# The tile's h in two PSUM banks, and all products of the up rows on TensorE in two further banks

## The chip, the cores and the metric

The kernel runs on one NeuronCore of a Trainium2 chip. The number is the device time of one execution in microseconds (us), lower is better. Engines are named as in the profile: PE is TensorE (PEld its weight loads), DVE is VectorE, ACT is ScalarE, POOL is GpSimd, SP is SyncE, which here only issues DMAs. All data is float32 unless a line says otherwise.

## The reference

Two blocks of a network run one after the other on 256 tokens of width 1024. The first block has two layers; a layer works on a sequence x and, in the first layer, also on a context of 256 tokens. Each ends in a lookup of experts (`_peer`), and that is the part the change touches. Every token picks 8 x 16 = 128 of 16384 experts, multiplies its vector h with each picked row of `peer_down`, and sums the picked rows of `peer_up`, weighted by gate and gelu:

```python
def one(args):
    hh, ee, gg = args
    a = jnp.einsum("tkd,td->tk", peer_down[ee], hh, preferred_element_type=jnp.float32)
    act = (gg * jax.nn.gelu(a)).astype(hh.dtype)
    return jnp.einsum("tk,tkd->td", act, peer_up[ee])
```

`ee` (token, 128) are the expert numbers from two top-16 searches per head, one over 128 + 128 scores and one over their 256 sums; `gg` is a softmax over the 16 best. The result is multiplied by a modulation vector and added to x. Around it stand an attention with 8 heads, a Fourier and a pooling branch, gates and output products. The second block (feed-forward, convolution, attention, feed-forward) follows the lookup and is not touched.

## The kernel before, in words

**Work and order.** A pass of one sequence through one layer is a run: `x0` and `c0` are sequence and context in layer 0, `x1` and `c1` in layer 1. `ORDER` is a list of stages written by hand; every engine walks the same list and does its share of each stage. There are six gathers, one per run (`x0`, `c0`, `x1`) and tile of 128 tokens (t = 0, 1), numbered G = 0 to 5. Each lasts 16 groups. Between the groups of a gather `ORDER` places stages of something else (beside): ranking, all of `c0` up to its scoring beside `x0`; the modulation of layer 1 (two 1 MB weight loads per group), ranking and the first stages of `x1` beside `c0`; ranking only beside `x1` t = 0, nothing beside `x1` t = 1.

**A group** handles 8 of a token's 128 experts. `rows` has eight slots of 128 x 1024. GpSimd's queue fetches eight rows of `peer_down` (one per token and slot, line 2079, 512 KB each), then eight of `peer_up`, into the same slots: down of group n, up of group n - 1, down of group n + 1 and so on. Before a down row goes into slot j, the up row there must have been used (`upv_done` and `upp_done`); before an up row goes there, the down row must have been used (`down_done`).

- VectorE, per group n: eight reductions of row times h (line 1643, one multiply-and-sum of 1024 elements each, counts `down_done`), three small operations for gelu, the stages beside, then eight accumulations of the left half of the up rows of group n - 1 into `accv` (line 1660, columns 0 to 511, counts `upv_done`), then `act8` of group n, for which it waits for ScalarE's tanh.
- ScalarE: eight diagonal matrices of `act8` of group n - 1 (line 1261, in four buffers `diag`, so each waits for the product four rows earlier), then its beside stages, then tanh of group n (line 1265).
- TensorE: the products of stages beside, then the right half of the up rows of group n - 1: `diag` times row, columns 512 to 1023, summed in PSUM bank 4 over the whole gather (line 847, counts `upp_done`). A float32 product shows as two passes in the trace.

At the end of a gather `fin` multiplies both halves with `mb`, the modulation vector that ScalarE has copied from PSUM, and adds them to x: four operations of 512 elements (lines 1697 to 1701). The next gather begins with a memset of `accv`.

**PSUM** has 8 banks of 512 float32 per partition. Bank 4 (`UPB`) holds the sum; every other product takes the next of the seven banks in `ROT` (`job`) and waits for the engine that empties it (`bank_free`). The attention of `c0` puts the scores of each tile (128 x 256) and each tile's transposed probabilities in a bank of its own.

## Time and profile before

| what | value |
|---|---|
| median of 3 runs | 4579.39 us (4568.43 to 4579.72) |
| profiled execution | 4569.33 us |
| its span on the core | 4567.2 us |
| PE, DVE busy | 3093.4 us, 2899.1 us |
| ACT, POOL busy | 961.5 us, 1820.7 us |
| mean granted TensorE clock | 0.821 of full |
| HBM read | 1153.99 MB, 253 GB/s over the span |

The page gives busy times over the whole span. The gathers run from about 434 us to 2310 us and from 2550 us to 3372 us, with the first stages, a stretch of modulation and layer 1, and the second block around them. Because stages with different limits alternate within a gather, the profile is best read in windows that begin with a group's first reduction on VectorE (line 1643). The granted clock is given as a part of 2.4 GHz; 0.50 is 1.2 GHz. A TensorE busy time is longer at the lower clock for the same work.

### The profile page before, as it was taken

What the parts mean: (1) busy time and instruction counts of PE and PEld (TensorE: products, weight loads), DVE (VectorE), ACT (ScalarE), POOL (GpSimd) and SP (SyncE); (2) the same over time, 40 slices, a digit from 0 to 9 for tenths busy, and PEclk for the clock granted to TensorE, in tenths of its full rate; (3) what the DMA queues carried; (4) which work ended last, traced back from release to release, by engine and by line L of the source; (5) the groups of instructions that cost most, each with busy time, mean ns of one, the idle gap of its engine ahead of it and who ended that gap; (6) DMA issues with size and microseconds to landing.
All of it is one profiled execution on the core that took longest, in us unless ns stands there. A gap on an engine that the chain in (4) does not pass through costs nothing.

```text
span 4567.2 us, 42252 instructions
## 1 busy us (share of the span) xinstructions
PE 3093.4 (68%) x12636; PEld 1964.9 (43%) x12636; DVE 2899.1 (63%) x5798; ACT 961.5 (21%) x1932; POOL 1820.7 (40%) x1732
## 2 busy tenths in 40 slices
PE   5996366688745544566788543344459878898789
PEld 2575022354511111123446311111139768797687
DVE  2215987566788777666642888776666566565365
ACT  1301012111111001111131111111123353333333
POOL 0001566566566555667620477777830000000000
PEclk7998677888867777787899766677679989999799
DMA  5434788899988888899943688899965504454244
GB/s 208 177 135 168 247 295 328 304 365 364 349 288 320 306 338 302 323 359 354 396 166 115 205 306 308 326 346 349 348 260 186 173 32 170 166 184 168 83 166 152
DMA packets 273573, 1157.15 MB, mean 253 GB/s; under 512 B 30848, under 2 KB 31616, under 8 KB 234496
## 3 DMA queue, kind: packets, MB, share of 16 engines
q0 software_dynamic: 221184, 805.40, 48.3%
q1 hardware_dynamic: 52224, 349.75, 21.2%
q8 instruction: 78, 1.28, 0.1%
q14 instruction: 87, 0.71, 0.0%
HBM read 1153.99 MB, written 1.05 MB: 253 GB/s over the span
## 4 chain that ended last, share of the span: by engine, by line
PE 40%; DVE 24%; DMA 20%; issue 9%; POOL 4%; ACT 2%; POOLq 0%; DVEq 0%; SPq 0%; ACTq 0%
DMA rows<-in_peer_up,iup 13%; PE ps L886 7%; PE ps L887 7%; PE ps L888 7%; DVE rows L1643 6%; DVE accv L1660 6%; DMA rows<-in_peer_down,idown 5%; PE ps L847 5%; POOL rows L2079 3%; PE ps L773 3%; PE ps L615 3%; PE ps L818 2%; PE ps L796 1%; PE ps L991 1%; DVE shared L1594 1%
## 5 line engine op out<-in xcount | busy, mean ns | idle before, releaser
L847 PE MATMUL ps<-rows,diag 128*128 128x512 f32 x1536 | 1021.3, 792 | 1182.7 <-DMA rows<-in_peer_up,iup 1139.9
L847 PEld LDWEIGHTS ps<-rows,diag 128*128 128x128 f32 x1536 | 320.2, 239 | 1864.3 <-DMA rows<-in_peer_up,iup 1336.6
L2079 POOL DMA_INDIRECT rows<-in_peer_down,idown x768 | 866.9, 1129 | 532.0 <-DVE accv L1660 269.3
L2079 POOL DMA_INDIRECT rows<-in_peer_up,iup x768 | 883.2, 1150 | 345.9 <-issue 185.1
L1660 DVE SCALAR_TENSOR_TENSOR accv<-rows,act,accv 128x512 f32<-128x512 f32 x768 | 577.4, 752 | 336.1 <-DMA rows<-in_peer_up,iup 295.7
L1261 ACT ACTIVATE diag<-ident,act 128x128 f32<-128x128 f32 x768 | 277.4, 396 | 2104.9 <-PE ps L847 1605.6
L1643 DVE CUSTOM_DVE_ANT_0 rows<-rows,h_in 128x1024 f32<-128x1024 f32 x512 | 612.3, 1225 | 89.2 <-DMA rows<-in_peer_down,idown 76.1
L886 PE MATMUL ps<-hT_hi,w_hi 128*128 128x256 f32 x1600 | 452.9, 283 | 16.5 <-DVE hT_lo L1758 16.5
L887 PE MATMUL ps<-hT_hi,w_lo 128*128 128x256 f32 x1600 | 452.9, 283 | 0.0
L888 PE MATMUL ps<-hT_lo,w_hi 128*128 128x256 f32 x1600 | 450.6, 282 | 0.0
L1643 DVE CUSTOM_DVE_ANT_0 rows<-rows,h_ctx 128x1024 f32<-128x1024 f32 x256 | 310.9, 1225 | 110.9 <-DMA rows<-in_peer_down,idown 106.3
L1745 DVE TENSOR_TENSOR w_lo<-wring,w_hi 128x2048 fp32r<-128x2048 f32 x120 | 275.0, 2292 | 142.9 <-ACT w_hi L1308 141.4
L886 PEld LDWEIGHTS ps<-hT_hi,w_hi 128*128 128x128 f32 x1600 | 306.2, 191 | 18.1 <-issue 18.1
L2084 POOL COPY idown<-idx 128x8 uint32 (+1 forms) x96 | 40.3, 420 | 666.7 <-DVE gates L1629 666.4
L887 PEld LDWEIGHTS ps<-hT_hi,w_lo 128*128 128x128 f32 x1600 | 304.0, 190 | 0.0
L888 PEld LDWEIGHTS ps<-hT_lo,w_hi 128*128 128x128 f32 x1600 | 303.9, 190 | 0.0
L1308 ACT ACTIVATE w_hi<-wring 128x2048 fp32r<-128x2048 f32 x120 | 229.4, 1912 | 130.4 <-DMA wring<-in_wdn 82.6
L773 PE MATMUL ps<-hT,wring 128*128 128x256 f32 x1152 | 253.0, 381 | 0.0
L773 PEld LDWEIGHTS ps<-hT,wring 128*128 128x128 f32 x1152 | 219.9, 191 | 38.2 <-issue 8.1
L818 PE MATMUL ps<-hT,wring 128*128 128x256 f32 x768 | 168.9, 379 | 2.0 <-ACT hT L1089 2.0
L818 PEld LDWEIGHTS ps<-hT,wring 128*128 128x128 f32 x768 | 144.8, 190 | 22.8 <-issue 3.9
L887 PE MATMUL ps<-w_hi,hid_lo 128*128 128x512 f32 x352 | 138.3, 393 | 0.0
(274 smaller groups left out, 3700.4 us busy)
## 6 DMA issues: line engine op xcount, KB each, us to landing
wring<-in_wgu SPq DMA_DIRECT2D x66, 1024.0 KB, 4.8
wring<-in_wmod SPq DMA_DIRECT2D x48, 1024.0 KB, 7.9
wring<-in_wG SPq DMA_DIRECT2D x36, 1024.0 KB, 7.8
wring<-in_wdn SPq DMA_DIRECT2D x33, 1024.0 KB, 4.8
wring<-in_wpq SPq DMA_DIRECT2D x24, 1024.0 KB, 5.7
rows<-in_wgu SPq DMA_DIRECT2D x22, 1024.0 KB, 4.8
wring<-in_wO SPq DMA_DIRECT2D x12, 1024.0 KB, 4.9
wring<-in_wout SPq DMA_DIRECT2D x12, 1024.0 KB, 4.8
```

What stands on the lines that cost most here:

```text
L773: last = pe.matmul(b[:, dt * TOK:(dt + 1) * TOK], w[:, k * 256 + dt * P:k * 256 + (dt + 1) * P], hT[:, k, :], start=(k == 0), stop=(k == K ...
L818: last = pe.matmul(b[:, hp * TOK:(hp + 1) * TOK], w[:, k * 256 + hp * P:k * 256 + (hp + 1) * P], hT[:, k, :], start=(k == 0), stop=(k == K ...
L847: pe.matmul(ps[:, UPB, :], diag[:, j % DIAGS, :], rows[:, j, UPV:D], start=(first and j == 0), stop=(last and j == GROUP - 1), skip_group_ ...
L886: pe.matmul(out_, lh[l_at], rh[r_at], start=start, stop=False)
L887: pe.matmul(out_, ll[l_at], rh[r_at], start=False, stop=False)
L888: return pe.matmul(out_, lh[l_at], rl[r_at], start=False, stop=stop)
L1261: act.activation(diag[:, j % DIAGS, :], ident[:, :], ACT.Copy, scale=act8[:, j:j + 1]).then_inc(diag_ready, 1)
L1308: act.activation(W2_HI[c % SLOTS2], W2[c % SLOTS2], ACT.Copy).then_inc(hi_ready, 1)
L1643: dve.tensor_tensor_reduce(out=rows[:, j, :], in0=rows[:, j, :], in1=h[s][:, t, :], scale=1.0, scalar=0.0, op0=ALU.mult, op1=ALU.add, accu ...
L1660: dve.scalar_tensor_tensor(accv[:, :], rows[:, j, 0:UPV], act8[:, j:j + 1], accv[:, :], ALU.mult, ALU.add).then_inc(upv_done, 1)
L1745: dve.tensor_tensor(W2_LO[c % SLOTS2], w, W2_HI[c % SLOTS2].bitcast(f32), ALU.subtract).then_inc(lo_ready, 1)
L2079: pool.indirect_dma_start(out=rows[:, j, :], out_offset=None, in_=table, in_offset=bass.IndirectOffsetOnAxis(ap=offs[:, j:j + 1], axis=0)) ...
```

## The change

Four things change at once. (1) ScalarE copies h of the tile into PSUM banks 6 and 7 (`h_ps`) at the start of a gather, and VectorE's reduction reads h from there. (2) TensorE multiplies both halves of an up row, into banks 4 and 5 (`up_sum`); VectorE's accumulation, `accv` and `upv_done` are gone, and `upp_done` alone frees a slot. (3) `fin` works on 1024 elements at a time, in two operations instead of four. (4) From the start of the first gather to the end of the fourth, and from the start of the fifth on, four banks are left for the stages beside (`ROT_GATHER`); the attention of `c0` therefore puts both tiles' scores in one bank and both tiles' transposed probabilities in one, with one maximum operation and one copy for both instead of two each.

```diff
         ROT = [0, 1, 2, 3, 5, 6, 7]
+        ROT_GATHER = [0, 1, 2, 3]
         UPB = 4
-        UPV = 512
+        TAKEN = [4, 5, 6, 7]
+        up_sum = ps[:, 4:6, :].rearrange("p b n -> p (b n)")
+        h_ps = ps[:, 6:8, :].rearrange("p b n -> p (b n)")
...
             def job(key):
-                b = ROT[rot[0] % len(ROT)]
+                b = banks[0][rot[0] % len(banks[0])]
...
                         pe.wait_ge(diag_ready, 8 * g + (P * G + j + 1))
-                        pe.matmul(ps[:, UPB, :], diag[:, j % DIAGS, :], rows[:, j, UPV:D], start=(first and j == 0), stop=(last and j == GROUP - 1),
-                                  skip_group_check=True).then_inc(upp_done, 1)
-
+                        for half in range(2):
+                            ins = pe.matmul(ps[:, UPB + half, :], diag[:, j % DIAGS, :], rows[:, j, half * 512:(half + 1) * 512],
+                                            start=(first and j == 0), stop=(last and j == GROUP - 1), skip_group_check=True)
+                        ins.then_inc(upp_done, 1)
+
+                if n0 == 0 and run != "c0" and t == 0:
+                    for b in TAKEN:
+                        taken_at[run, b] = uses[b]
+                        uses[b] += 1
+                    banks[0] = ROT_GATHER
...
+                if n0 == 0:
+                    s = RUNS[run][0]
+                    if G in (0, 4):
+                        taken(act, run, TAKEN[2:4])
+                    else:
+                        act.wait_ge(down_done, P * G)
+                    act.wait_ge(mark["h"], norm_mark(run, 1, 2))
+                    for half in range(2):
+                        at_evac(act, ("bh", run, 1, half))
+                    for half in range(2):
+                        cols = slice(half * 512, (half + 1) * 512)
+                        act.activation(h_ps[:, cols], h[s][:, t, cols], ACT.Copy).then_inc(h_copied, 1)
...
+                if nk == 2:
+                    b = at_mm(dve, ("s", run, i)).rearrange("p (t n) -> p t n", t=TT)
+                    c = 2 * (i % 2)
+                    dve.tensor_reduce(nmax[:, c:c + 2], b, axis=AX.X, op=ALU.max, negate=True).then_inc(mark["nmax"], 2)
...
-                if n0 == 0:
-                    v(dve.memset(accv[:, :], 0.0))
 
                 def down(g, first=False):
 
+                    if first:
+                        dve.wait_ge(h_copied, 2 * G + 2)
                     for j in range(GROUP):
                         dve.wait_ge(row_in[j], (16 * (32 * G + 1)) if first else 32 * g + 16 * (32 * G))
-                        dve.tensor_tensor_reduce(out=rows[:, j, :], in0=rows[:, j, :], in1=h[s][:, t, :], scale=1.0, scalar=0.0,
+                        dve.tensor_tensor_reduce(out=rows[:, j, :], in0=rows[:, j, :], in1=h_ps, scale=1.0, scalar=0.0,
                                                  op0=ALU.mult, op1=ALU.add, accum_out=a8[:, j:j + 1]).then_inc(down_done, 1)
...
-                def up(g, last=False):
-                    for j in range(GROUP):
-                        dve.wait_ge(row_in[j], (16 * (32 * G + 32)) if last else 32 * g + (16 * (32 * G + 3)))
-                        if isinstance(g, int) and g == 0 and j == 0:
-                            dve.wait_ge(act_ready, GROUPS * G + 1)
-                        else:
-                            dve.wait_ge(upv_done, 8 * g + (P * G + j))
-                        dve.scalar_tensor_tensor(accv[:, :], rows[:, j, 0:UPV], act8[:, j:j + 1], accv[:, :], ALU.mult, ALU.add).then_inc(upv_done, 1)
-
...
-                dve.wait_ge(upv_done, P * (G + 1))
-                v(dve.tensor_tensor(accv[:, :], accv[:, :], mb[:, 0:UPV], ALU.mult))
                 dve.wait_ge(upp_done, P * (G + 1))
-                v(dve.tensor_tensor(mb[:, UPV:D], ps[:, UPB, :], mb[:, UPV:D], ALU.mult))
-                v(dve.tensor_tensor(x[s][:, t, 0:UPV], x[s][:, t, 0:UPV], accv[:, :], ALU.add))
-                dve.tensor_tensor(x[s][:, t, UPV:D], x[s][:, t, UPV:D], mb[:, UPV:D], ALU.add).then_inc(mark["fin"], 1)
+                v(dve.tensor_tensor(mb[:, :], up_sum, mb[:, :], ALU.mult))
+                dve.tensor_tensor(x[s][:, t, :], x[s][:, t, :], mb[:, :], ALU.add).then_inc(mark["fin"], 1)
                 at_mark(dve, "fin", run, t + 1)
+                if run != "x0" and t == TT - 1:
+                    for b in TAKEN:
+                        dve.sem_inc(bank_free[b], 1)
```

What stands in a row on the engines, at the places where it changes. On TensorE in the first gather, rows 2 to 6 of the first group's up products before, and rows 2 to 4 now; `diag_ready` and `row_in2` are the semaphores of the diagonal and of the fetched row.

```order
308 L847 MATMUL ps<-rows,diag 128x512 [waits diag_ready,row_in2]
309 L847 MATMUL ps<-rows,diag 128x512 [waits diag_ready,row_in3]
310 L847 MATMUL ps<-rows,diag 128x512 [waits diag_ready,row_in4]
311 L847 MATMUL ps<-rows,diag 128x512 [waits diag_ready,row_in5]
312 L847 MATMUL ps<-rows,diag 128x512 [waits diag_ready,row_in6]
```

```order
310 L872 MATMUL ps<-rows,diag 128x512 [waits diag_ready,row_in2]
311 L872 MATMUL ps<-rows,diag 128x512
312 L872 MATMUL ps<-rows,diag 128x512 [waits diag_ready,row_in3]
313 L872 MATMUL ps<-rows,diag 128x512
314 L872 MATMUL ps<-rows,diag 128x512 [waits diag_ready,row_in4]
315 L872 MATMUL ps<-rows,diag 128x512
```

Every row of `peer_up` now has two products, and only the second tells the others that its slot is free. On VectorE at the end of the last gather, from the last group's gelu to its `act8`, before and now (line 1666 waits for ScalarE's tanh):

```order
3985 L1651 TENSOR_TENSOR g<-g,a 128x8 [waits gelu_step]
3986 L1660 SCALAR_TENSOR_TENSOR accv<-rows,act,accv 128x512 [waits upv_done,row_in0]
3987 L1660 SCALAR_TENSOR_TENSOR accv<-rows,act,accv 128x512 [waits upv_done,row_in1]
3988 L1660 SCALAR_TENSOR_TENSOR accv<-rows,act,accv 128x512 [waits upv_done,row_in2]
3989 L1660 SCALAR_TENSOR_TENSOR accv<-rows,act,accv 128x512 [waits upv_done,row_in3]
3990 L1660 SCALAR_TENSOR_TENSOR accv<-rows,act,accv 128x512 [waits upv_done,row_in4]
3991 L1660 SCALAR_TENSOR_TENSOR accv<-rows,act,accv 128x512 [waits upv_done,row_in5]
3992 L1660 SCALAR_TENSOR_TENSOR accv<-rows,act,accv 128x512 [waits upv_done,row_in6]
3993 L1660 SCALAR_TENSOR_TENSOR accv<-rows,act,accv 128x512 [waits upv_done,row_in7]
3994 L1666 SCALAR_TENSOR_TENSOR g<-th,a 128x8 [waits gelu_th]
3995 L1672 TENSOR_TENSOR act<-g,gates 128x8 [waits upv_done,diag_ready,gelu_step]
```

```order
3297 L1711 TENSOR_TENSOR g<-a 128x8 [waits down_done]
3298 L1713 TENSOR_SCALAR g<-g 128x8 [waits gelu_step]
3299 L1715 TENSOR_TENSOR g<-g,a 128x8 [waits gelu_step]
3300 L1721 SCALAR_TENSOR_TENSOR g<-th,a 128x8 [waits gelu_th]
3301 L1726 TENSOR_TENSOR act<-g,gates 128x8 [waits diag_ready,gelu_step]
3302 L1747 TENSOR_TENSOR mb<-ps,mb 128x1024 [waits bank_free1,upp_done,bank_free0,act_ready]
```

The eight accumulations are gone, and VectorE comes to the wait for tanh right after gelu. On ScalarE between the fifth and the sixth gather, before and now (lines 1261 and 1306 are the diagonals, 1089 and 1124 the copy of `mb`):

```order
551 L1261 ACTIVATE diag<-ident,act 128x128 [waits upp_done,act_ready]
552 L1261 ACTIVATE diag<-ident,act 128x128 [waits upp_done] x7
553 L1089 ACTIVATE mb<-ps 128x512 [waits mm_done] x2
554 L1265 ACTIVATE th<-g 128x8 [waits gelu_in]
555 L1261 ACTIVATE diag<-ident,act 128x128 [waits upp_done,act_ready]
```

```order
561 L1306 ACTIVATE diag<-ident,act 128x128 [waits upp_done,act_ready]
562 L1306 ACTIVATE diag<-ident,act 128x128 [waits upp_done] x7
563 L1124 ACTIVATE mb<-ps 128x512 [waits mm_done] x2
564 L1323 ACTIVATE ps<-h_in 128x512 [waits bank_free2,bank_free3,h,down_done]
565 L1323 ACTIVATE ps<-h_in 128x512
566 L1310 ACTIVATE th<-g 128x8 [waits gelu_in]
```

Two copies of h have come between the copy of `mb` and the first tanh of the next gather.

## Rows read from the trace of the kernel before

**Rows 1.** The page: busy shares, then costly groups (busy us, mean ns | idle before).
```profile
PE 3093.4 (68%) x12636; PEld 1964.9 (43%) x12636; DVE 2899.1 (63%) x5798; ACT 961.5 (21%) x1932; POOL 1820.7 (40%) x1732
...
L2079 POOL DMA_INDIRECT rows<-in_peer_down,idown x768 | 866.9, 1129 | 532.0 <-DVE accv L1660 269.3
...
L1660 DVE SCALAR_TENSOR_TENSOR accv<-rows,act,accv 128x512 f32<-128x512 f32 x768 | 577.4, 752 | 336.1 <-DMA rows<-in_peer_up,iup 295.7
```
**Rows 2.** Windows, groups 1 to 14 of each gather: length, busy us, clock, DMA, GB/s.
```profile
469.00:875.50 406.50, 219.68 (x451) 81.60 (x452) 318.34 (x725) 64.93 (x203) 268.10 (x249) 0.71 0.84 294
944.50:1371.00 426.50, 308.99 (x950) 178.80 (x948) 302.64 (x647) 61.39 (x171) 266.45 (x256) 0.83 0.91 341
1436.20:1868.80 432.60, 229.36 (x440) 72.06 (x440) 308.05 (x652) 47.22 (x140) 260.18 (x249) 0.73 0.85 322
1928.80:2289.00 360.20, 238.01 (x640) 122.24 (x640) 236.44 (x432) 61.64 (x179) 252.62 (x254) 0.81 0.95 368
2579.10:2954.40 375.30, 155.47 (x224) 47.31 (x224) 312.65 (x688) 42.41 (x130) 270.39 (x249) 0.67 0.87 307
3003.20:3339.80 336.60, 155.43 (x224) 46.22 (x224) 230.52 (x407) 41.97 (x127) 271.33 (x253) 0.69 0.95 348
```
**Rows 3.** Windows, single groups: PE, PEld, DVE, ACT, POOL, clock, DMA, GB/s.
```profile
595.50:625.40 29.90, 12.36 (x16) 3.44 (x16) 27.98 (x83) 2.98 (x9) 18.78 (x18) 0.61 0.81 277
652.20:689.10 36.90, 32.19 (x89) 14.63 (x87) 18.87 (x43) 7.66 (x22) 22.43 (x23) 0.91 0.92 347
1179.20:1221.10 41.90, 41.90 (x188) 34.10 (x187) 22.59 (x55) 7.28 (x19) 19.95 (x22) 1.00 0.91 343
...
2268.60:2289.00 20.40, 9.91 (x16) 3.68 (x16) 16.48 (x29) 2.99 (x10) 16.07 (x18) 0.67 1.02 407
```
**Rows 4.** Timeline in the sixth stretch (start, us); then line 2079's DMA to landing there.
```profile
3102.34 1.22 DVE L1643 CUSTOM_DVE_ANT_0 rows<-rows,h_in 128x1024 f32<-128x1024 f32 x1
3102.39 1.99 POOL L2079 DMA_INDIRECT rows<-in_peer_down,idown  x1 [0.30 <-issue]
...
3114.52 0.93 POOL L2079 DMA_INDIRECT rows<-in_peer_up,iup  x1 [0.30 <-issue]
...
DMA to landing us min/median/max: 5.1/6.0/6.8
```
**Rows 5.** Waits of POOL in the third stretch: us in total, times, longest.
```profile
POOL rows L2079 <- DVE accv L1660: 76.2, 34, 14.5
```
**Rows 6.** Windows of line 847 (PE, PEld, clock, DMA, GB/s); then a burst's start.
```profile
1134.40:1141.20 6.80, 6.79 (x16) 2.85 (x15) 1.00 0.70 272
3134.80:3140.50 5.70, 5.61 (x7) 2.36 (x8) 0.51 0.99 386
3140.50:3150.60 10.10, 5.03 (x10) 1.27 (x8) 1.00 0.94 350
3351.00:3371.00 20.00, 18.07 (x31) 5.40 (x32) 0.89 0.96 377
3134.89 8.39 PE L847 MATMUL ps<-rows,diag 128*128 128x512 f32 x12 [11.78 <-DMA rows<-in_peer_up,iup]
```
**Rows 7.** Groups of instructions with their shapes: busy us, mean ns | idle before.
```profile
L1697 DVE TENSOR_TENSOR accv<-accv,mb 128x512 f32<-128x512 f32 x6 | 4.2, 693 | 13.4 <-ACT mb L1089 13.3
L1699 DVE TENSOR_TENSOR mb<-ps,mb 128x512 f32<-128x512 f32 x6 | 4.1, 691 | 0.2
L1554 DVE TENSOR_REDUCE nmax<-ps 128x1 f32<-128x256 f32 x16 | 6.0, 418 | 0.7 <-PE ps L743 0.6
L1089 ACT ACTIVATE mb<-ps 128x512 f32<-128x512 f32 x18 | 10.1, 593 | 105.4 <-PE ps L540 105.4
```
**Rows 8.** Windows: line 847 at 652.2; nine groups' sums, all work, then line 847.
```profile
652.20:689.10 36.90, 10.74 (x16) 3.26 (x16) 0.91 0.92 347
...
sum 286.70, PE 240.03 PEld 151.74 DVE 189.19 ACT 42.99 POOL 171.14; mean PE 26.67 PEld 16.86 DVE 21.02 ACT 4.78 POOL 19.02
...
sum 286.70, PE 87.23 PEld 29.78; mean PE 9.69 PEld 3.31
```

More of the change, by code:

```diff
@@ L476, in release, with taken @@
             ins.then_inc(bank_free[job_bank[key]], 1)
+        def taken(eng, run, banks):
+            for b in banks:
+                eng.wait_ge(bank_free[b], taken_at[run if run == "x1" else "x0", b])
         def norm_mark(run, k, n):
@@ L739, in att @@
                             at_evac(pe, ("qT", run, t, hq))
-                if i < H:
+                if i < H and nk == 2:
+                    b = job(("s", run, i))
+                    for t in range(TT):
+                        last = pe.matmul(b[:, t * TOK:(t + 1) * TOK], qT[0:QK, i, t * P:(t + 1) * P], kT[0:QK, i, 0:TOK], start=True, stop=True)
+                    ended(last, ("s", run, i))
+                elif i < H:
                     for t in range(TT):
```

62 lines of the change are left out of this document (39 added, 23 removed).

## The prediction

> **What bounds the kernel now.** I read the page first: engines, the 40 slices, the chain and the costly groups. TensorE is busy 68% and VectorE 63% of the span, so neither average names a limit. The costly groups are the six gathers' own: fetches on GpSimd's queue, products on VectorE's and TensorE's [rows 1]. So I cut each gather into its groups (of eight fetches down and eight up) and looked at groups 1 to 14 of each, six stretches that together hold 2337.7 of the 4567.2 us [rows 2]. Mean period of a group: 29.0, 30.5, 30.9, 25.7, 26.8 and 24.0 us (stretch over 14).
>
> Three kinds of group are to be seen [rows 3]. Where ranking runs beside (595.5), VectorE works 27.98 of 29.9 us: VectorE is the limit. Where dense products run beside (1179.2), TensorE works 41.9 of 41.9 us. Where nothing runs beside (the sixth stretch), no engine is full; there GpSimd issues almost without a pause: 336.6 us for 14 x 16 fetches is 1.50 us each, and a fetch takes 0.94 us when VectorE leaves it alone, up to 1.99 us when line 1643 runs back to back, plus a gap of 0.30 us [rows 4]. The best group of all, 20.4 us, has DMA at 407 GB/s [rows 3].
>
> **What the change removes.** Per group VectorE loses eight accumulations of 0.752 us (577.4 us over 768) [rows 1]. The next starts about 0.85 us after the last, so 6.8 us per group. That is worth 6.8 us only in groups that VectorE fills. Elsewhere it shortens a path: a slot is refilled only when VectorE and TensorE have both finished its up row, and in the third stretch GpSimd waited 76.2 us for line 1660 [rows 5]. After the change TensorE alone frees the slot.
>
> **What it moves to TensorE.** An up row is now two products, four passes. Sixteen passes at the full clock took 6.79 us, 0.424 each [rows 6]; so 1.70 us a row and 13.6 us a group at 2.4 GHz, twice that at 1.2 GHz. In a lone burst the clock is not full at once: it stood at 0.51 for the 5.7 us after 3134.8 and at 1.00 for the 10.1 us behind them, and TensorE had been idle for 11.78 us ahead [rows 6]. With 5.7 us at half (1.7 rows) and 6.3 rows at 1.70 us, a burst is 16.4 us. Estimate of a lone group from this: first landing 5.1 to 6.0 us after its issue (least and median of [rows 4]; 5.3, since refills paced by TensorE leave fewer transfers in flight), burst 16.4, and 1.3 for the fetch that is issued between the last freed slot and the next up row's own: 23.0 us. The other floors lie below: sixteen fetches at 1.24 us are 19.8 us, with the two copies of indices a little more, and 8.39 MB at 407 GB/s are 20.6 us. So **the limit of a lone group moves from GpSimd's issue to the ring of slot, landing and TensorE burst**, and the gain there is only 24.0 to 23.0.
>
> **h in PSUM.** The 768 reductions keep their length: a 128x512 TENSOR_TENSOR took 693 ns with both inputs in SBUF and 691 ns with one in PSUM [rows 7]. Bounds: 0 and +0.1 us each on a path that then has slack (VectorE falls to about 16 us in a lone group with its waits), so 0. The Trainium skill, VectorE: DVE Perf Modes, section on the TRN2 errata, gives VectorE a larger fixed part for a PSUM source (120 cycles against 58). By it the 768 reductions would cost 0.065 us more each, 50 us in all, and the pair of 691 and 693 ns speaks against it. What the move should bring is on GpSimd: fetches beside line 1643 are the long ones [rows 4], while the mean over all is 1.13 to 1.15 us [rows 1]; at 0.94 each group gets back 16 x 0.21 = 3.4 us of GpSimd time. The trace has no reduction with h in PSUM, so the bound is 0 to 3.4 us a group; I take most of it, since without it the lone group stays at about 24. The Trainium skill, SBUF — State Buffer, section "SBUF: two separate sides", says that VectorE with two SBUF inputs holds a port pair shared with GpSimd, against a GpSimd operation that reads SBUF. By that rule the whole 3.4 us would come back, and the 0.94 to 1.99 us agree with its direction.
>
> **Sum by stretch** (14 groups each; dense work beside read as TensorE's busy time less line 847's [rows 2, 8]).
> First, 406.5: five groups (469.0 to 625.4) are full of VectorE, as 595.5 is, and lose 6.8 us each: 156.4 - 34 = 122.4; one (652.2) with 32.2 - 10.7 = 21.5 us of dense work gets 21.5 + 13.6 = 35.1; eight at 23 are 184. Sum 341.5, **-65**.
> Second, 426.5: nine groups, 286.7 us long, carry 240.0 - 87.2 = 152.8 us of dense work [rows 8] and get 152.8 + 9 x 13.6 = 275; the other five (139.8) get 4 x 23 and, one of them full of VectorE at 33.2, 26.4: 118. Sum 393, **-33**. A group such as 1179.2 gets longer by its 16 added passes, 6.8 us, to 48.7.
> Third, 432.6: 322 GB/s over it are 139.3 MB, because the modulation's weights load beside; at 380 GB/s, between the 368 of the fourth stretch and the 407 of the best group, 366 us: **-66**, limited by DMA.
> Fourth, 360.2 at 368 GB/s: 132.5 MB at 380 are 349: **-11**.
> Fifth, 375.3: VectorE without line 1660 works 312.7 - 112 x 0.752 = 228 us, well under 14 x 23 = 322: **-53**.
> Sixth, 336.6: 322, **-15**.
> Together -243. Against it: at a gather's end the last two bursts now follow one another, 27.2 us plus 2.9 at half clock against the 20 us in which TensorE worked off 31 passes from 3351.0 [rows 6]; less what was hidden, some 7 us at five ends: +35. The end's four VectorE operations of 0.69 us and a memset become two of 1024 elements, about 1.2 us each: -5 over six. ScalarE's copies of h, 2 x 0.59 us by its copies of mb [rows 7], run beside these operations: 0; uncovered they are 1.2 us x 6 = 7. The copy stands in front of the gather's first reduction and behind the last group's diagonals and mb on ScalarE; fetches are queued on GpSimd and don't wait. The attention beside the second stretch (8 heads): two reductions of 0.418 us [rows 7] become one of about 0.69, two exponentials now start behind both maxima: between -2 and +4, taken 0. Four banks instead of seven for the stages beside: nothing in the trace shows the wait; bounds 0 and 2 us for each of some 25 groups with TensorE work beside; I take 20. Sum: -243 + 35 - 5 + 20 = **-193**. The profiled execution took 4569.33 us (span 4567.2), the median of the runs is 4579.39, within their spread; so 4569 - 193 = 4376, said as **4380**.
>
> **Rivals.**
> A, GpSimd keeps its long fetches (h in PSUM does not help it). The lone groups stay at 24 instead of 23, in some 45 groups: 4425. For it: a reduction still reads and writes SBUF. Against: the long ones lie beside line 1643, both of whose inputs are in SBUF [rows 4].
> B, TensorE becomes the limit beside dense work beyond the sum, and the four banks make its stages wait for evacuations that ScalarE does only between its diagonals: 3 us more in 25 to 30 groups, 4460. For: 1179.2 is already full.
> C, better than the sum: bursts of 16 us keep the clock up over the pauses and dense work fills them; lone groups reach 21.3 (5.3 + 13.6 + 1.3 is 20.2, and GpSimd's floor lies beside it), and the third stretch runs at 400 GB/s: 4380 - 50 x 1.5 = 4305.
> D, slower: TensorE stays at 1.2 GHz through the bursts. Four stretches (first, third, fifth, sixth) average 27.7 us a group; less 6.6 for landing and issues, a burst may last 21.1 us before it costs time. With r rows at half, 13.6 + 1.7r = 21.1 gives r = 4.4, so it decides if the clock stays down for 15 us of each burst instead of 5.7. All rows at half make 33.8 us a group: (33.8 - 27.7) x 56 = +342, less the 44 of the second and fourth, plus the 50 of ends and banks, 4917. A clock that returns at 5.7 us in [rows 6] speaks against it.
> E, no change: the stalls taken from VectorE come back as waits for DMA in every stretch. Only the fourth stretch, at 368 GB/s, looks so.
>
> **How the numbers follow.** Forecast 0.46, A 0.16, B 0.17, C 0.13, D and lesser mishaps beyond it 0.05, E 0.03. The range leaves out D, E and the far ends of B and C: 4290 to 4480. About 0.3% is what a measurement of this kernel can tell from no change; beyond it faster has 0.91 (forecast, A, B, C, less a little of B), same 0.04, slower 0.05.
>
> **What would show it.** No line 1660; line 847's successor with 3072 passes; fetches at 0.94 us throughout (else A). Mean period in the sixth stretch near 23 with bursts of about 16 us, the clock rising some 5 us into them (else C or D). The ranking groups of the first stretch near 23 to 26.5 instead of 30 to 33; a group like 1179.2 at 48; the modulation groups at about 26 with DMA near 380 GB/s. TensorE waiting on bank_free in stages beside would be B. The forecast is wrong if a landing takes over 7 us once the queue is denser, for that enters each period whole.

## The result, and the profile after

The changed kernel takes 4408.6 us (median of 4 runs, 4405.7 to 4418.0), the kernel before 4579.6 in the same series. The ratio is 0.9634, 95% interval 0.9611 to 0.9656: 168 us less. The span of the profiled execution is 4406.8 us against 4567.2, so 160 us are to be explained from the traces. The forecast was 193 us less.

The page of the changed kernel, busy shares and the costly groups that answer to [rows 1] (busy us, mean ns | idle before, releaser), and last the products up as the page of before has them:

```profile
PE 3532.5 (80%) x14172; PEld 2263.5 (51%) x14172; DVE 2322.0 (53%) x5004; ACT 990.4 (22%) x1936; POOL 1495.9 (34%) x1732
...
L872 PE MATMUL ps<-rows,diag 128*128 128x512 f32 x3072 | 1466.2, 638 | 599.2 <-DMA rows<-in_peer_up,iup 597.9
...
L1707 DVE CUSTOM_DVE_ANT_0 rows<-rows,ps 128x1024 f32<-128x1024 f32 x768 | 915.0, 1220 | 238.8 <-DMA rows<-in_peer_down,idown 229.1
L2129 POOL DMA_INDIRECT rows<-in_peer_down,idown x768 | 730.5, 951 | 665.0 <-PE ps L872 497.0
L2129 POOL DMA_INDIRECT rows<-in_peer_up,iup x768 | 724.8, 944 | 360.5 <-DVE a L1707 156.8
...
L847 PE MATMUL ps<-rows,diag 128*128 128x512 f32 x1536 | 1021.3, 792 | 1182.7 <-DMA rows<-in_peer_up,iup 1139.9
```

VectorE lost 577 us of work, TensorE got 1536 more passes but only 439 us more busy time, because a pass now takes 638 ns on average, and took 792 by the page of before: the granted clock, a mean over the span, rose from 0.821 to 0.907. GpSimd's fetches fell from 1.13 (down) and 1.15 us (up) to 0.95 and 0.94, and the reduction with h in PSUM takes 1220 ns, as before (1.22 us [rows 4]).

Groups 1 to 14 of the six gathers, in the columns of [rows 2] (length, busy us of PE, PEld, DVE, ACT and POOL, clock, DMA share, GB/s):

```profile
464.80:826.60 361.80, 267.84 (x661) 123.87 (x662) 233.22 (x605) 65.61 (x195) 216.57 (x248) 0.87 0.90 331
903.40:1309.70 406.30, 367.93 (x1174) 219.40 (x1172) 220.02 (x536) 64.92 (x171) 216.69 (x252) 0.95 0.94 357
1369.10:1728.30 359.20, 294.11 (x662) 107.62 (x663) 224.38 (x540) 51.90 (x141) 215.44 (x249) 0.95 0.99 391
1785.20:2138.20 353.00, 302.63 (x855) 162.90 (x856) 152.08 (x322) 65.03 (x179) 213.43 (x251) 0.93 0.98 375
2448.90:2780.60 331.70, 215.81 (x436) 92.13 (x437) 229.88 (x576) 46.41 (x129) 216.28 (x248) 0.84 0.93 345
2840.10:3171.30 331.20, 215.36 (x436) 92.04 (x437) 148.40 (x294) 45.99 (x126) 212.90 (x250) 0.84 0.95 352
```

| stretch | 1 | 2 | 3 | 4 | 5 | 6 | sum |
|---|---|---|---|---|---|---|---|
| before | 406.5 | 426.5 | 432.6 | 360.2 | 375.3 | 336.6 | 2337.7 |
| forecast | 341.5 | 393 | 366 | 349 | 322 | 322 | 2094 |
| after | 361.8 | 406.3 | 359.2 | 353.0 | 331.7 | 331.2 | 2143.2 |

The stretches lost 194.5 us; the rest of the program, where only the ends of gathers change, got 34 us longer. Single groups of the changed kernel, same columns: ranking beside (514.6), dense products beside in the first gather (610.0 and 674.5) and in the second (1126.8), modulation beside (1521.8), nothing beside (3052.2):

```profile
514.60:542.10 27.50, 15.94 (x32) 6.80 (x32) 25.45 (x65) 3.46 (x10) 17.92 (x19) 0.88 0.94 347
610.00:653.30 43.30, 42.19 (x132) 21.43 (x131) 12.76 (x36) 9.63 (x26) 18.25 (x21) 1.00 0.80 282
674.50:705.70 31.20, 27.09 (x84) 13.86 (x82) 12.07 (x26) 8.26 (x24) 18.73 (x22) 1.00 0.99 374
1126.80:1176.40 49.60, 49.60 (x199) 36.25 (x198) 16.43 (x48) 7.61 (x19) 18.70 (x22) 1.00 0.82 299
1521.80:1547.40 25.60, 21.33 (x49) 7.06 (x48) 17.23 (x48) 3.21 (x9) 15.40 (x18) 1.00 1.02 410
3052.20:3076.10 23.90, 15.51 (x34) 6.68 (x33) 10.55 (x21) 3.31 (x9) 15.45 (x19) 0.86 0.95 348
```

**The lone group, step by step.** In the timeline at 3056 us (start, length, idle before and its releaser) the last row of one burst is used at 3057.4, and the next burst begins at 3065.81:

```profile
3058.23 0.94 POOL L2129 DMA_INDIRECT rows<-in_peer_down,idown  x1 [0.78 <-DVE a L1707]
3059.47 0.94 POOL L2129 DMA_INDIRECT rows<-in_peer_up,iup  x1 [0.30 <-issue]
...
3065.81 2.07 PE L872 MATMUL ps<-rows,diag 128*128 128x512 f32 x2 [8.39 <-DMA rows<-in_peer_up,iup]
```

0.8 us until the freed slot's fetch is issued (the program waits there for `upp_done` of TensorE; the reduction that the profile names is not what this fetch waits for), 1.24 until the first fetch up is, 6.3 until that has landed: 8.4 us in which TensorE stands. Then the burst, in windows of line 872 alone (length, PE, PEld, clock, DMA share, GB/s): its first 3.8 us at a clock of 0.60, the other 11.8 at 1.00.

```profile
3065.80:3069.60 3.80, 3.79 (x6) 1.76 (x7) 0.60 1.00 386
3069.60:3081.40 11.80, 11.69 (x28) 4.90 (x26) 1.00 0.97 371
```

8.4 + 15.5 = 23.9 us, against 5.3 + 16.4 + 1.3 = 23.0 in the forecast.

### The profile page after: what moved, and what is told of

The parts are those of the page before. It is cut to its first block, busy times and chain, and to the rows that moved or that the text cites. A ratio compares the mean times of both kernels' runs of the same rounds, so it can differ in the third digit from the quotient of the medians.

```text
span 4406.8 us, 43688 instructions
## 1 busy us (share of the span) xinstructions
PE 3532.5 (80%) x14172; PEld 2263.5 (51%) x14172; DVE 2322.0 (53%) x5004; ACT 990.4 (22%) x1936; POOL 1495.9 (34%) x1732
## 4 chain that ended last, share of the span: by engine, by line
PE 57%; DMA 15%; DVE 12%; issue 8%; POOL 6%; ACT 2%; POOLq 0%; SPq 0%; DVEq 0%; ACTq 0%
PE ps L872 16%; DMA rows<-in_peer_up,iup 9%; PE ps L921 7%; PE ps L922 7%; PE ps L923 7%; POOL rows L2129 6%; PE ps L797 5%; DMA rows<-in_peer_down,idown 5%; PE ps L631 4%; DVE rows L1707 3%; PE ps L842 3%; PE ps L820 2%; PE ps L1026 1%; DMA wring<-in_wmod 1%; PE ps L774 1%
## 5 line engine op out<-in xcount | busy, mean ns | idle before, releaser
L872 PE MATMUL ps<-rows,diag 128*128 128x512 f32 x3072 | 1466.2, 638 | 599.2 <-DMA rows<-in_peer_up,iup 597.9
L872 PEld LDWEIGHTS ps<-rows,diag 128*128 128x128 f32 x3072 | 621.2, 206 | 1426.7 <-issue 1000.1
L1707 DVE CUSTOM_DVE_ANT_0 rows<-rows,ps 128x1024 f32<-128x1024 f32 x768 | 915.0, 1220 | 238.8 <-DMA rows<-in_peer_down,idown 229.1
L2129 POOL DMA_INDIRECT rows<-in_peer_down,idown x768 | 730.5, 951 | 665.0 <-PE ps L872 497.0
L2129 POOL DMA_INDIRECT rows<-in_peer_up,iup x768 | 724.8, 944 | 360.5 <-DVE a L1707 156.8
L1306 ACT ACTIVATE diag<-ident,act 128x128 f32<-128x128 f32 x768 | 301.0, 400 | 1921.9 <-PE ps L872 1846.1
L921 PE MATMUL ps<-hT_hi,w_hi 128*128 128x256 f32 x1600 | 452.6, 283 | 16.4 <-DVE hT_lo L1808 16.4
L1721 DVE SCALAR_TENSOR_TENSOR g<-th,a 128x8 f32<-128x8 f32 x96 | 16.5, 172 | 547.8 <-ACT th L1310 547.3
L2134 POOL COPY idown<-idx 128x8 uint32 (+1 forms) x96 | 19.1, 199 | 680.3 <-DVE gates L1693 679.7
L921 PE MATMUL ps<-w_hi,hid_hi 128*128 128x512 f32 x352 | 138.0, 392 | 0.0
```

Of the source, the lines that this page charges most:

```text
L872: ins = pe.matmul(ps[:, UPB + half, :], diag[:, j % DIAGS, :], rows[:, j, half * 512:(half + 1) * 512], start=(first and j == 0), stop=(la ...
L921: pe.matmul(out_, lh[l_at], rh[r_at], start=start, stop=False)
L1306: act.activation(diag[:, j % DIAGS, :], ident[:, :], ACT.Copy, scale=act8[:, j:j + 1]).then_inc(diag_ready, 1)
L1707: dve.tensor_tensor_reduce(out=rows[:, j, :], in0=rows[:, j, :], in1=h_ps, scale=1.0, scalar=0.0, op0=ALU.mult, op1=ALU.add, accum_out=a8[ ...
L2129: pool.indirect_dma_start(out=rows[:, j, :], out_offset=None, in_=table, in_offset=bass.IndirectOffsetOnAxis(ap=offs[:, j:j + 1], axis=0)) ...
```

## The experiments

Ratios are to the kernel before, run on the same chip. Experiments 1 to 4 shared one chip, 5 to 7 a second, 8 to 11 a third, 12 had a fourth; why that matters is told under 8.

**1. h in SBUF again.**

```diff
-  dve.tensor_tensor_reduce(out=rows[:, j, :], in0=rows[:, j, :], in1=h_ps, ...
+  dve.tensor_tensor_reduce(out=rows[:, j, :], in0=rows[:, j, :], in1=h[s][:, t, :], ...
```

> The changed kernel, but VectorE's reductions read h from SBUF again; the copies of h into PSUM stay, so nothing else moves. Theory R (the ring of slot, landing and TensorE burst sets a lone group): GpSimd's fetches go back from 0.95 to about 1.13 us, but 16 x (1.13 + 0.30) + 0.4 = 23.3 us is still under the 24.0 us of a lone group. Only two fetches lie on the ring (the last one down and the first one up), so a lone group gets 0 to 0.5 us longer: sixth stretch 331 to 338 us, the whole kernel 4410 to 4440. Rival P (the issue of fetches on GpSimd is what the move of h relieved and carries the gain): every group gets 16 x 0.2 = 3.2 us longer, sixth stretch near 376, the kernel near 4409 + 84 x 3 = 4660, or at least above 4500.

Measured: 4524.4 us, ratio 0.9867 (0.9839 to 0.9895). The page's groups of fetches, and GpSimd's timeline in a ranking group of this kernel, then in the same group of the changed kernel:

```profile
L2129 POOL DMA_INDIRECT rows<-in_peer_down,idown x768 | 811.8, 1057 | 550.5 <-PE ps L872 305.5
L2129 POOL DMA_INDIRECT rows<-in_peer_up,iup x768 | 869.6, 1132 | 326.3 <-issue 194.0
...
554.97 1.96 POOL L2129 DMA_INDIRECT rows<-in_peer_up,iup  x1 [0.30 <-DVE a L1707]
557.23 1.98 POOL L2129 DMA_INDIRECT rows<-in_peer_up,iup  x1 [0.30 <-issue]
559.52 0.94 POOL L2129 DMA_INDIRECT rows<-in_peer_up,iup  x1 [0.30 <-PE ps L872]
```

```profile
546.75 0.94 POOL L2129 DMA_INDIRECT rows<-in_peer_up,iup  x1 [0.30 <-DVE a L1707]
547.99 0.94 POOL L2129 DMA_INDIRECT rows<-in_peer_up,iup  x1 [0.30 <-DVE a L1707]
549.24 0.94 POOL L2129 DMA_INDIRECT rows<-in_peer_up,iup  x1 [0.31 <-DVE a L1707]
```

So the bank for h does shorten the fetches, by 226 us in the sum of all 1536. It is worth much more time than theory R gave (at most 31 us) and less than rival P's 250, though the time lies above P's bound of 4500: ratio 0.9867 against 0.9623 of experiment 4, on the same chip, is 112 us (experiment 4 differs from the changed kernel by a small edit), and 0.9639 of experiment 8, on another chip, puts it at 104. Theory R was wrong in counting only the two fetches of the lone group's ring. The third stretch, 357.1 us in experiment 4, took 385.4 here, the second 426.1 for 406.7, a lone group 24.7. Groups of every kind got longer. My reading is that a long fetch beside the reductions delays each fetch behind it, up and down; how much of the time comes this way was not measured apart.

**2. The left half back on VectorE,** h still in PSUM: `accv` and the eight `scalar_tensor_tensor` of a group return, line 872 multiplies columns 512 to 1023 only.

> The changed kernel with the left half of the up rows back on VectorE (accv, 768 accumulations of about 0.75 us); h stays in PSUM, four banks for the stages beside stay. Theory R: the burst on TensorE in a lone group shrinks to 16 passes, some 8 to 9 us, so the ring is 8.4 + 9 = 17 us and no longer the limit; what remains is the issue of 16 fetches, 16 x 1.24 + 0.4 = 20.2 us, or DMA at the best seen 407 GB/s, 20.6 us. Sixth stretch about 14 x 21 = 294 us instead of 331, ends of gathers 10 us shorter in the last two. The ranking groups of the first stretch go back to 30 to 33 us (+34 us), the dense ones lose their added passes. Whole kernel 4380 to 4440. Rival S (the gain comes from taking VectorE's accumulations away everywhere): the sixth stretch stays at 331 or goes up, and the kernel is at 4500 or more.

Measured: 4561.9 us, ratio 0.9942 (0.9923 to 0.9962). The sixth stretch fell, to 317.2, but not to 294; the first took 393.1, the third 427.1 and the fifth 378.5. Rival S had the right size for the whole and the wrong sign for the lone gather. The second stretch, where the dense groups were to lose their added passes, took 437.4 us against 406.7 in experiment 4. This ran on a disturbed chip (see under 8): on another one theory R's 294 us were reached, 290.3 in experiment 11, with the same division of work in the sixth gather. The third stretch is the surprise: there VectorE was 71% busy before, and taking its accumulations away is worth 68 us all the same (70 against experiment 4, on the same chip).

**3. Both parts back.** Experiments 1 and 2 together.

> Both parts undone: left half on VectorE and h read from SBUF. Against the kernel before, what is left is: four banks instead of seven for the stages beside, the merged scores and probabilities of the attention, the two unused copies of h, and a fin with one addition of 1024 elements. So it measures the price of four banks. My prediction took 20 us for it: 4600. If the banks cost nothing: 4575 to 4585. Rival B (TensorE's stages beside wait for banks that ScalarE empties late): 3 us in each of 25 to 30 groups, 4655 to 4670. Together with the two runs above it gives the four corners of h in PSUM and left half on TensorE; if the two parts only add up, (both back) - (left on VectorE) equals (h in SBUF) - (changed kernel).

Measured: 4605.0 us, ratio 1.0027 (1.0007 to 1.0047): four banks with the merged attention, the two unused copies of h and the other `fin` cost 12 us (3 to 22), not 20. Of the six stretches the second grew most, 437.0 us against 426.5 in the profile of before; but that profile is of another chip, and the whole span of this one is 35 us longer than its, so the place of the cost is not shown. The group with the most dense work (1179.2 in [rows 3], 41.9 us) took 47.3 us here, and 42.0 in experiment 10, which has the four banks too. The four corners are 0.9634 (changed; 0.9639 in experiment 8), 0.9867, 0.9942 and 1.0027. They don't add up: h in PSUM alone brings 0.0085, with the left half on TensorE 0.023; the left half on TensorE brings 0.016 without and 0.031 with h in PSUM. My reading is that each part takes away what stood beside the other. The corner of the changed kernel is from other chips; with 0.9623 of experiment 4, on the chip of the other three, the two larger numbers are 0.024 and 0.032. How much of the difference is the disturbance of that chip was not measured.

**4. TensorE kept busy in the pause.**

```diff
...
+                def pause(n):
+                    for k in range(8 if warm and not is_group(n, 0) and not is_group(n, GROUPS - 1) else 0):
+                        pe.matmul(ps[:, wb, :], ident[:, :], keysT[:, 0:512], start=True, stop=True, skip_group_check=True)
...
```

`warm` holds in the fifth and the sixth gather; `pause(n)` follows each burst.

> The changed kernel; in the lone groups of the fifth and sixth gather TensorE multiplies eight unneeded products of 512 columns into an unused bank after each burst of up rows, 6.8 us at the full clock, in the 8.4 us in which it was idle. Theory R with the clock as part of the burst: TensorE is not idle long enough to fall to 1.2 GHz, the burst is 13.6 us instead of 15.5, and a lone group takes 22.0 to 22.5 us: sixth stretch 310 us instead of 331, kernel about 4388. Rival N (the half-clock part of the burst lies beside landings that are late anyway, or the added products delay the next burst): sixth stretch 331 us or more, kernel 4409 or more.

Measured: 4416.8 us, ratio 0.9623 (0.9598 to 0.9647). The sixth stretch took 326.5 us, the fifth 336.5 (331.7 in the changed kernel, on another chip). Line 872 alone in one of its shorter groups:

```profile
3038.80:3060.40 21.60, 13.12 (x32) 5.60 (x31) 1.00 0.93 358
```

The clock was 2.4 GHz over this whole burst (mean of the sixth stretch 0.95) and the burst fell below 14 us, as said; but the mean group is 23.3 us, not 22. Direction right in the sixth stretch, size not reached, and this chip has a disturbance (see under 8) that can be larger than the difference.

**5. and 6. Fetches up ahead of fetches down.** GpSimd's queue: D0 to D5, U0, D6, U1, D7, U2 to U7 (experiment 5), and the same with four (experiment 6).

```diff
+                LEAD = 2
...
+                    for step in range(GROUP + GROUP - LEAD):
+                        if step >= GROUP - LEAD:
+                            up(gu, pu, ahead=ahead_u, js=(step - GROUP + LEAD,))
+                        if step < GROUP:
+                            down(gd, pd, ahead=ahead_d, js=(step,))
...
```

> The changed kernel with another order on GpSimd's queue: the first two fetches of up rows go ahead of the last two fetches down (D0 to D5, U0, D6, U1, D7, U2 to U7 instead of D0 to D7, U0 to U7); all work and all other orders stay. Theory R (a lone group is the ring: last up row used, last fetch down issued, first fetch up issued behind it, landing 6.3 us, burst 15.5 us): U0 is issued behind D5 and not behind D7, which is two TensorE rows, 3.4 us, earlier, and the shorter pause of TensorE leaves less of the burst at half clock. The lone group falls from 24.0 to 20.6 to 21 us, where DMA (8.39 MB at 407 GB/s) and the issue of 16 fetches (20.2 us) lie: sixth stretch 290 to 300 us instead of 331, DMA at 395 GB/s or more there. All lone and half-lone groups gain, so the kernel falls to 4270 to 4330. Rival D (the sixth stretch is at the DMA's own limit for these fetches: its engines are 95% busy at 352 GB/s): it stays at 325 us or more, landings get longer by what the issue gained, and the kernel stays at 4390 or more.

> As the run before, but four fetches of up rows go ahead of the last four fetches down. Theory R: the ring gives 24.0 - 6.8 = 17 us, which is no longer the limit in a lone group, so against the run before nothing more is gained there (within 0.5 us a group, 20.6 to 21); a first fetch up that waits for the first reduction now holds back four fetches down, which may cost 0 to 1 us. Kernel within 0.5% of the run before. Rival D: no change from the changed kernel either, 4390 to 4420. If the ring was still the limit in the run before, this one is clearly faster, by 1% or more.

Measured: 4471.5 us, ratio 0.9752 (0.9735 to 0.9770), and 4707.7 us, ratio 1.0269 (1.0251 to 1.0286). Theory R fell in both. Rival D's numbers came out in experiment 5 (over 4390 us, sixth stretch 328.1), but experiment 10 rules its cause out. In the sixth stretch of experiment 5 the burst did begin 3 us sooner after a group's first reduction (10.5 us, before 13.6), yet that group takes 23.7. GpSimd's timeline there:

```profile
3109.31 0.94 POOL L2129 DMA_INDIRECT rows<-in_peer_down,idown  x1 [0.30 <-DVE a L1707]
3110.55 0.94 POOL L2129 DMA_INDIRECT rows<-in_peer_up,iup  x1 [0.30 <-DVE a L1707]
...
3123.13 0.94 POOL L2129 DMA_INDIRECT rows<-in_peer_up,iup  x1 [1.58 <-DVE a L1707]
3124.37 0.94 POOL L2129 DMA_INDIRECT rows<-in_peer_down,idown  x1 [0.30 <-issue]
```

The last two fetches down now stand behind fetches up that wait for reductions (`DVE a L1707`); D7 lands late, its reduction ends late, U7 waits for it, and the next D0 stands behind U7. One ring was shortened and another, through the same queue, took its place. Beside ranking it is worse: the first stretch took 412.0 us (377.3 in experiment 7, on the same chip), and GpSimd's fetches waited 105.2 us for reductions there, 65.4 in the changed kernel. My reading is that the queue had the rows of the next group ready there and now has them late. With four fetches ahead every stretch got longer, the sixth to 361.9 us.

**7. VectorE's left half in the last gather alone.**

> The changed kernel, but in the last gather alone, which has nothing beside, the left half of the up rows is on VectorE, as before; h stays in PSUM, the order of fetches stays. From the run with all left halves on VectorE: its sixth stretch took 317 us against 331 and its last end was some 7 to 10 us shorter. So 20 to 25 us less than the changed kernel: about 4385. If instead the gain of that run in the sixth stretch came from its neighbours, nothing changes: 4409 within 5 us.

Measured: 4415.2 us, ratio 0.9633 (0.9615 to 0.9651), nothing gained. The sixth stretch was 321.3 us, 10 less, but the first 377.3, 15 more, with the same instructions there as in the changed kernel. VectorE stood still in its ranking code, 1 to 2.6 us at a time, and the profile names as releaser another core or an unknown queue.

**8. to 11. One chip, four kernels:** the changed kernel again; with 96 tiny memsets at VectorE's start; without the left half's product; and a choice of places for VectorE:

```diff
...
+        def left_on_pe(G, n, rolled=False):
+
+            return not (G == 5 or (isinstance(n, int) and (n >= 14 or (G == 0 and n in (6, 8)))))
...
```

`n` is the group whose up rows are multiplied; they are used in the stretch of group n + 1.

> The changed kernel itself once more, beside the three below on the same chip. It is the measure of two things seen in the runs so far: its first stretch took 361.8 us, but 372 to 377 us in two kernels whose work, order and VectorE program there are the same, because VectorE stood still for 1 to 2.6 us at a time in the ranking code with nothing to wait for. If that belongs to the kernel (where its code lies), this profile shows again no such pauses and 362 us in the first stretch. If it belongs to the chip or the hour, it shows them now, 370 to 378 us. The ratio stays at 0.963 in both cases, within 0.003.

> The changed kernel with 96 tiny VectorE operations (a memset of 128 x 4 each) put at its very start, where VectorE waits for its first loads; they add under 10 us there and shift all of VectorE's code behind them. If the pauses in the ranking code come from where the code lies, they appear or move here, and the first stretch differs from that of the unshifted kernel on the same chip by 5 us or more. If they have another cause, both have the same first stretch within 3 us. Kernel: 4409 to 4450.

> The changed kernel without the product of the left half of the up rows (but for the first row of a gather): TensorE has 8 products of 16 passes less a group, and nothing takes their place, so the left half of the lookup's sum is left out. Fetches, reductions and their order stay. Theory R (the ring of slot, landing and TensorE burst): the burst falls to some 9 us and the ring to 17 to 18 us; then the issue of 16 fetches is next, 16 x 1.24 + 0.4 = 20.2 us, and the sixth stretch takes 283 to 290 us at 405 GB/s or more. Theory D (DMA can't carry more than some 370 GB/s of these fetches over many groups; the runs so far had at best 368 GB/s in lone groups): it stays at 22.3 to 23 us a group, 312 to 322 us, whatever TensorE does.

> The changed kernel with the left half of the up rows on VectorE at chosen places only: all of the last gather, the last two groups (14 and 15) of each other gather, and groups 6 and 8 of the first gather, beside the dense stages of which TensorE had no time left. The rest stays on TensorE. From the run with all left halves on VectorE: the ends of gathers lose 7, 0, 0, 8, 8 and 10 us, the last stretch 10 to 14, and the first 8 + 5 in two groups. Sum 45 us: 4365 (4350 to 4385), ratio 0.953. If the pauses of VectorE in the ranking code come with it, up to 30 us of that are lost again: 4395. If the ends don't move, because landings set them and not TensorE, 4385.

Measured: 0.9639 (0.9626 to 0.9652), 0.9629 (0.9616 to 0.9643), 0.9073 (0.9059 to 0.9087) at 4156.0 us, and **0.9480 (0.9463 to 0.9497) at 4340.9 us**, the best kernel of the study and 24 us better than expected: the sixth stretch gave 41 us where 10 to 14 were said.

Experiments 8 and 9 had first stretches of 363.6 and 361.7 us and no such wait, like the first profile: neither the kernel nor this shift of its code is the cause. The profiles of the kernel before, of the changed kernel's first run and of 8 to 11 hold no wait that ends by an unknown releaser, those of 1 to 7 and 12, on three other chips than 8 to 11, all do, 3 to 37 of them each. The chip of the first run is not on record, and each of the four chips was used at one time only, so the chip and the hour can't be told apart. Two kernels with the same instructions in the last gather show what it costs there, here the waits of GpSimd's fetches in the sixth stretch (us in total, times, longest) of experiment 7, then of experiment 11, and the windows:

```profile
POOL rows L2173 <- issue: 64.2, 192, 2.5
POOL rows L2173 <- DVE a L1729: 15.6, 13, 3.8
POOL rows L2173 <- remote: 10.6, 3, 4.5
```

```profile
POOL rows L2173 <- issue: 36.2, 121, 1.8
POOL rows L2173 <- DVE accv L1746: 19.4, 59, 2.5
```

```profile
2861.60:3182.90 321.30, 140.80 (x224) 46.08 (x224) 230.03 (x406) 42.82 (x126) 218.25 (x250) 0.71 0.96 363
```

```profile
2825.60:3115.90 290.30, 137.57 (x224) 48.56 (x224) 228.00 (x408) 41.98 (x127) 221.12 (x252) 0.74 1.02 403
```

31 us in one stretch, for equal work. So ratios of different chips here are not comparable below some 30 us, and experiments 1 to 7 and 12 may understate what their kernels do on a quiet chip; stretches with equal work show it for 4 and 7 (first stretch 372.2 and 377.3 for 361.8) and 12. The median of the kernel before differed by 11 us at most between the chips.

Experiment 10 settles what holds the lone group. Its sixth stretch:

```profile
2641.00:2929.10 288.10, 136.97 (x226) 48.38 (x226) 149.43 (x295) 47.28 (x130) 214.78 (x252) 0.74 1.02 406
```

and GpSimd's queue in it, where nearly all fetches follow one another at 1.24 to 1.28 us:

```profile
2813.87 0.94 POOL L2129 DMA_INDIRECT rows<-in_peer_up,iup  x1 [0.31 <-issue]
2815.11 0.94 POOL L2129 DMA_INDIRECT rows<-in_peer_up,iup  x1 [0.30 <-issue]
2816.36 0.94 POOL L2129 DMA_INDIRECT rows<-in_peer_up,iup  x1 [0.31 <-issue]
```

With half the passes the lone group is 20.5 us (mean 20.6), so TensorE's burst was in its ring. Now GpSimd issues almost without a pause: its 214.8 us of work and 73.5 us in 224 gaps, 0.33 us each on average, fill the 288.1. DMA carries 406 GB/s over 14 groups, so theory D is out; but its share is 1.02 and half of the fetches now land 6.9 us or more after their issue, where it was 6.0, so DMA may be near its limit too. Experiment 11 reaches 20.7 us with the whole sum computed, VectorE doing the left half. Its other gains: the sixth gather's stretch 290.3 for 331.2; group 7 of the first gather 36.4 us for 43.2 and group 9 28.9 for 31.2; the ends of the fourth and fifth gather (from the first reduction of group 15 to that of the next gather) 287.9 and 40.7 for 294.1 and 49.0. The ends of the second and third did not get shorter (44.4 and 47.8 for 42.2 and 46.5).

**12. Experiment 11 with TensorE kept busy in the fifth gather.** The edit of experiment 4, after the bursts of groups 0 to 13 of that gather.

> The kernel with VectorE's left halves at the ends and in the last gather (the best so far, ratio 0.948), and in the fifth gather alone TensorE multiplies eight unneeded products of 512 columns into an unused bank after each burst of up rows of groups 0 to 13, as in the earlier run with a busy pause; the sixth gather has none. In the fifth gather a group takes 23.6 us on average, TensorE 15 to 16.5 us of it, the first part of a burst at 1.2 GHz. Theory R: without the half-clock part the burst is 13.6 us, ScalarE has its last diagonal and the tanh behind it 2 to 3 us sooner, and a group takes 21 to 22.2 us: fifth stretch 295 to 312 us instead of 330, kernel 4310 to 4325, ratio 0.943. In the earlier run the clock did stay full but the group only fell to 23.3 us; GpSimd and VectorE stood still there at times with nothing to wait for. Rival Q: something else than the clock holds the group (landings that get longer as the burst gets shorter), fifth stretch 325 to 335 us, ratio 0.948.

Measured: 4385.7 us, ratio 0.9558 (0.9533 to 0.9583). The fifth stretch, then the sixth, which has the same instructions as in experiment 11:

```profile
2471.00:2796.00 325.00, 288.26 (x650) 124.69 (x651) 229.68 (x576) 44.98 (x131) 217.24 (x248) 0.97 0.94 351
2848.50:3166.90 318.40, 140.40 (x224) 49.03 (x224) 229.55 (x407) 43.15 (x127) 224.03 (x251) 0.69 0.96 367
```

The unchanged sixth stretch is 28 us longer than on the other chip, the first, unchanged too, 14, and the waits with an unknown releaser are back (ScalarE's diagonals: 38.3 us in 16). The clock rose to 0.97 in the fifth stretch and that became 5 us shorter in spite of it, but the experiment does not decide between R and Q. What the half clock costs stays open.

## Where the prediction held and where it failed

- **What bounds the lone group: right, 1 us too low.** The ring of slot, landing and burst is what experiment 10 shows. The term that was mis-sized is the landing, taken at 5.3 us, between the least and the median of [rows 4], measured 6.3: the median of 6.0 was the better value. Fewer fetches were indeed in flight when the first fetch up was issued, 2.9 on average over the sixth stretch against 3.5 before, but it landed 6.2 us after its issue (median), before 5.9. Freeing and issue took 2.1 us, not 1.3. The burst was better than said, 15.5 us instead of 16.4, as its part at the lower clock is shorter, 3.8 us at 0.60, than in [rows 6], 5.7 at 0.51; there TensorE had been idle for 11.8 us and not 8.4, and whether that is the reason no run shows. Over the fifth and sixth stretch: 19 us short of the forecast.
- **Ranking groups: right.** 23.1 to 27.4 us in the first stretch where 23 to 26.5 was said, and 29.8 to 33.4 before. The fifth stretch lost 44 of the 53 us forecast.
- **Third stretch: right,** 359.2 us at 391 GB/s for 366 at 380. That DMA is the limit there fits experiment 10: with half of TensorE's passes the stretch took 354.4 us.
- **Dense groups: the step that failed.** For the first stretch I took one group with dense work, at dense work plus 13.6 us, and "eight at 23". Four of the eight, groups 9 to 12, have dense work beside them too and took 31.2, 26.1, 26.8 and 25.3 us: 17 of the 20 us by which the first stretch missed. Counting their dense work (8.8, 3.9, 6.3 and 6.3 us before) by my own rule would not have mended it, since 8.8 + 13.6 is still under 23. What the rule lacks is that stages beside can stand in the ring itself. Between the bursts at 738.5 and 765.3 us (TensorE, VectorE, GpSimd, TensorE):

```profile
755.22 1.03 PE L759 MATMUL ps<-kvmem,shared 96*128 96x256 f32 x4
756.38 0.69 DVE L1611 TENSOR_REDUCE nmax<-ps 128x2 f32<-128x512 f32 x1 [5.26 <-PE ps L759]
758.63 1.21 DVE L1707 CUSTOM_DVE_ANT_0 rows<-rows,ps 128x1024 f32<-128x1024 f32 x1
760.75 0.94 POOL L2129 DMA_INDIRECT rows<-in_peer_up,iup  x1 [3.62 <-DVE a L1707]
765.25 5.17 PE L872 MATMUL ps<-rows,diag 128*128 128x512 f32 x8 [4.85 <-DMA rows<-in_peer_up,iup]
```

  TensorE makes the attention's scores behind its burst, VectorE takes their maximum and goes on with the softmax, and only then reduces the first row down, for which GpSimd's first fetch up waits. So TensorE's burst begins 9.9 us after the last one ended, and not 8.4. In group 9 a weight load of 1 MB runs beside, and the fetches up landed 8.8 us after their issue (median). Groups 6 to 8 together, with the one that I did count, took 84.7 us for 81.1. In the second stretch the nine dense groups took 287 us for 275, with TensorE busy 279 of them. A group such as 1179.2 was right in kind: 49.6 for 48.7, TensorE 49.6 busy.
- **h in PSUM: right in direction and for the fetches, wrong in worth.** No cost on the reduction (1220 ns), fetches at 0.95 us. But rival A, the case without that help, was priced at 45 us, one microsecond in each lone group; experiment 1 puts it at 104 to 112. The prediction followed it only through GpSimd's total time, where there was slack, and experiment 1 shows stretches of every kind longer. Behind the measurement: the Trainium skill, SBUF — State Buffer, section "SBUF: two separate sides", has a VectorE operation with two SBUF inputs and a GpSimd operation that reads SBUF exclude each other on a shared port pair, for the whole instruction. By that rule a fetch beside back-to-back reductions waits for one of 1.22 us to end, and an estimate from it is 0.94 to 2.16 us. The trace agrees: the rows show 1.96 and 1.98, and 0.94 with one input in PSUM. No run separates this rule from another effect of the second SBUF input.
- **Ends of gathers and fin: right in the sum, partly by luck.** +35 and -5 forecast, +34 measured outside the stretches. The ends alone, from group 15 on, got 45 us longer: the fifth went from 38.2 to 49.0, the sixth (to its last product) from 32.2 to 43.1, the fourth from 273.5 to 294.1, with 33 us of line 872 in it, the first from 58.3 to 65.2, while the second and third got 5 shorter together. Against it stand 10 us less elsewhere, where the sum had 5 for `fin`: the first gather starts 4.2 us sooner, the first groups of the gathers take 3.4 less, and the part behind the last gather 2.8.
- **Four banks:** 20 taken, 12 measured (3 to 22), with the rest of experiment 3's edit in it.
- **Rivals.** B holds a part of the miss, in the first two stretches, by its dense work and not by its banks: TensorE's waits for ScalarE's copies out of PSUM (lines 1089 and 1124) fell from 10.4 to 1.9 us in the first stretch. C did not happen: the lone group stayed at 24.0. D (clock down through bursts) is refuted, 11.8 of 15.6 us ran at 2.4 GHz. E is refuted by the result.

The sum of these: first +20, second +13, third -7, fourth +4, fifth +10, sixth +9 us over their forecasts, less the 20 us set aside for banks, and +4 outside. That is the 33 us between 193 and 160.

## What to carry to other kernels

When work moves from one engine to another, cost it group by group against that engine's own window, and choose the side for each place: TensorE for the left half where VectorE ranks or modulation loads run, VectorE where nothing or dense products run beside, was worth a further 1.6% over the uniform move (0.948 for 0.964, on one chip). A stage beside that stands ahead of the work on which the next fetch waits lengthens the ring, however idle the engines are. If a GpSimd queue issues the DMAs, try one input of VectorE's long operations in PSUM, and don't put a fetch that waits for a result ahead of one that could go. Run the kernel that you compare with on the same chip, and look for waits without a releaser before you believe a difference of half a per cent.

## What the runs showed of the hardware that I had not expected

- 16 fetches of 512 KB, in 128 rows of 4 KB, ran at 403 to 406 GB/s over whole stretches of 290 us; 352 at a DMA share of 0.95 was not a limit.
- In the runs on three of the four chips GpSimd stood still for up to 4.5 us at a time, VectorE for up to 5.8 and ScalarE for up to 21, each wait ended by a releaser that the profile doesn't know. Of two kernels with equal work in one gather, the one with such waits took 31 us more there; the medians of the kernel before lie within 11 us on all chips. The cause is open.
- GpSimd's fetches beside VectorE's reductions took 1.96 to 1.98 us with both inputs of the reduction in SBUF and 0.94 with one in PSUM; that one operand was worth 0.0085 of the time in one version of the kernel and 0.023 in another.
